# Memory key and value projection woven into the sliding attention's block with its norms, and row norms joined to the projections behind them

## The reference

```python
def memory_kv(mem, lw):
    m = rmsnorm(mem, lw['mem_in_norm_g'])
    k = rmsnorm((m @ lw['w_mk']).reshape(B, M, MEM_HEADS, MEM_HD), lw['mem_k_norm_g'])
    v = (m @ lw['w_mv']).reshape(B, M, MEM_HEADS, MEM_HD)
    return k, v
...
    sq = rmsnorm(sq.reshape(B, T, SWA_HEADS, SWA_HD), lw['swa_q_norm_g'])
    sk = rmsnorm(sk.reshape(B, T, SWA_KV_HEADS, SWA_HD), lw['swa_k_norm_g'])
    h = x + jnp.concatenate([out_a, out_b, out_c], axis=-1) @ lw['w_o']
    h = h + memory_attend(rmsnorm(h, lw['norm_mem_g']), mem_k, mem_v, lw)
    u, ffn_buf_new = causal_dwconv(rmsnorm(h, lw['norm_ffn_g']) @ lw['w_up'], ffn_buf, lw['w_ffn_conv'])
```

## Time and profile before

| | us |
|---|---|
| median of 3 runs | 2190.31 (2185.15 to 2190.46) |
| the profiled execution | 2190.62 |
| its span | 2189.4 |
| TensorE busy | 1968.3 (90%) |
| VectorE busy | 1039.8 (47%) |
| ScalarE busy | 680.0 (31%) |
| GpSimd busy | 530.5 (24%) |

### The profile page before, as it was taken

How to read it: one execution, slowest core, us unless ns; L and a number is a source line. 1 busy time by engine, 2 the same in 40 slices (tenths; PEclk the granted TensorE clock), 3 DMA queues, 4 the chain that set the end, 5 groups by cost and what they waited for, 6 DMA issues and landing times. The chain is left out here.

```text
span 2189.4 us, 28444 instructions
## 1 busy us (share of the span) xinstructions
PE 1968.3 (90%) x10881; PEld 1799.7 (82%) x10881; DVE 1039.8 (47%) x1344; ACT 680.0 (31%) x1216; POOL 530.5 (24%) x453
## 2 busy tenths in 40 slices
PE   3899999889856987699998897999999999999997
PEld 3889889889745776599886687999999999999995
DVE  4224555746542211511341215666666757576665
ACT  4114663226542314311310314322223222222222
POOL 3000221024311606200211502323323223233230
PEclk9999999989976998799999998999999999999998
DMA  3121212141120304210223201212120111112012
GB/s 117 42 61 31 61 30 62 59 137 49 55 74 1 135 10 163 78 39 1 77 97 134 77 1 49 58 29 57 29 57 29 52 34 35 51 29 57 29 39 94
DMA packets 126933, 127.01 MB, mean 58 GB/s; under 512 B 10389, under 2 KB 109310, under 8 KB 126686
## 3 DMA queue, kind: packets, MB, share of 16 engines
q1 hardware_dynamic: 122238, 120.89, 17.8%
q10 hardware_dynamic: 3714, 4.76, 0.7%
q0 software_dynamic: 896, 0.19, 0.0%
HBM read 109.86 MB, written 15.96 MB: 57 GB/s over the span
## 5 line engine op out<-in xcount | busy, mean ns | idle before, releaser
L2732 PE MATMUL ffn_banks<-h_hi,up_hi 128*128 128x384 f32 x1056 | 352.9, 334 | 1.8 <-PEq L116 1.8
L2732 PE MATMUL ffn_banks<-h_hi,up_lo 128*128 128x384 f32 x1056 | 353.0, 334 | 0.0
L2732 PE MATMUL ffn_banks<-h_lo,up_hi 128*128 128x384 f32 x1056 | 352.8, 334 | 0.0
L2907 DVE TENSOR_TENSOR h<-h,ffn_banks 128x512 f32<-128x512 f32 x396 | 272.4, 688 | 146.4 <-PE ffn_banks L2767 142.2
L2877 DVE SCALAR_TENSOR_TENSOR ffn_conv_out<-ffn_conv_in,vec,ffn_conv_out 128x1168 f32<-128x1168 f32 x88 | 206.7, 2349 | 128.3 <-ACT ffn_conv_out L2798 122.5
L706 PE MATMUL proj_banks<-x_hi,in_w_hi 128*128 128x384 f32 (+1 forms) x648 | 222.2, 343 | 4.3 <-DVE room L1071 4.3
L706 PE MATMUL proj_banks<-x_lo,in_w_hi 128*128 128x384 f32 (+1 forms) x648 | 218.1, 337 | 0.0
L706 PE MATMUL proj_banks<-x_hi,in_w_lo 128*128 128x384 f32 (+1 forms) x648 | 217.9, 336 | 0.0
L2732 PEld LDWEIGHTS ffn_banks<-h_hi,up_hi 128*128 128x128 f32 x1056 | 198.2, 188 | 2.9 <-issue 2.0
L2732 PEld LDWEIGHTS ffn_banks<-h_lo,up_hi 128*128 128x128 f32 x1056 | 198.2, 188 | 0.9
L2732 PEld LDWEIGHTS ffn_banks<-h_hi,up_lo 128*128 128x128 f32 x1056 | 198.2, 188 | 0.0
(11 more groups left out here) (395 smaller groups left out, 3501.9 us busy)
## 6 DMA issues: line engine op xcount, KB each, us to landing
up_raw<-in_w_up SPq DMA_DIRECT2D x44, 512.0 KB, 6.2
in_w_raw<-in_w_in SPq DMA_DIRECT2D x22, 512.0 KB, 3.7
down_raw<-in_w_down SPq DMA_DIRECT2D x22, 512.0 KB, 3.7
mem_k_one<-in_cache_mem_k SPq DMA_DIRECT2D x8, 1024.0 KB, 4.9
spill<-mixT SPq DMA_DIRECT2D x10, 576.0 KB, 4.0
wo_w_raw<-in_w_o SPq DMA_DIRECT2D x8, 512.0 KB, 3.8
h<-in_x_prompt SPq DMA_DIRECT2D x8, 512.0 KB, 7.3
mkv_w_raw<-in_w_mk SPq DMA_DIRECT2D x8, 512.0 KB, 4.0
```

Source lines behind the costliest of these rows:

```text
L2732: ins = nc.tensor.matmul(banks[:, NP * s + p, 0:TC], wt[:, s, k, :], x[:, k, TC * p:TC * p + TC], start=(n == 0), stop=(n == 3 * KD - 1))
L2907: nc.vector.tensor_tensor(to, to, banks[:, d_bank[n % 5], :], ALU.add).then_inc(added, 1)
```

## The change

- `late_norms`, `window_attention` and `memory_kv` become one block, `window_and_memory`. In it the memory rows' norm is done beside the key and query norms, and the 192 products of the memory projection are cut into 64 units of three products, which TensorE takes in portions (`UNITS_AT`) between the scores and the outputs of the attention's tiles. One bank takes the groups of eight units one after the other; ScalarE copies each group out (`rows_out`). The weights come in 16 pairs of 128 x 512; ScalarE makes the high parts, GpSimd the low parts of the even pairs, VectorE those of the odd ones.
- The sample tile comes first. Its scores with the old windows are made by 32 products with queries masked for one sequence each, accumulated in the bank.
- Roots in this block are made by log and exp; the key norm gets one refining step on VectorE.
- Turned keys go to memory and are loaded again, with the values, in the block of the query projection.
- `norm_turn` before the query projection and before the FFN goes away; `NormParts` does the same steps inside the product's block. TensorE turns the first eight pieces, and then one piece ahead of each product of the first column; the products of the first column wait for their low part. The first two weight tiles' high parts move from GpSimd to ScalarE, ahead of and in the middle of the norm's high parts. In the query projection the later weights' low parts move from VectorE to GpSimd.
- The FFN's old rows are stored to memory in the input projection and loaded in the FFN's block; masks and buffers share room with others.

The diff, cut. The loops over `NT` at the end of `window_and_memory` are, in this order, those of TensorE, VectorE, ScalarE and GpSimd.

```diff
+class NormParts:
+    GROUP, RING = 3, 4
...
+    def turn(self, pe, i):
+        g, k = divmod(i, KD)
+        pe.wait_ge(self.scaled, self.GROUP * (g + 1))
+        if i >= self.RING:
+            pe.wait_ge(self.low, i - self.RING + 1)
...
+    def on_scalar(self, act, half_way):
+        for i in range(NP * KD):
+            if i == NP * KD // 2:
+                half_way()
+            self.high_part(act, i)
+
+    def on_vector(self, dve):
+        self.inverse(dve)
+        self.scale(dve, 0)
+        for i in range(NP * KD):
+            if i % KD == KD // 2 and i // KD + 1 < NP:
+                self.scale(dve, i // KD + 1)
+            self.low_part(dve, i)
+
+    def first_third(self, pe):
+        for i in range(KD):
+            self.turn(pe, i)
+
+    def before_product(self, pe, p, k):
+        i = KD * p + k + KD // 2
+        if KD <= i < NP * KD:
+            self.turn(pe, i)
+        pe.wait_ge(self.low, KD * p + k + 1)
...
+PAIRS, PAIR_RING, RAW_RING = 2 * KD, 5, 4
+UNITS_FIRST = KD
+UNITS_AT = [(4, 4)] * 5 + [(2, 2)] * 3 + [(4, 0)]
+ROWS_AT = {0: 1, 1: 2, 2: 3, 3: 4, 4: 5, 6: 6, 8: 7}
+PAIRS_FIRST = 4
+PAIRS_AT = {0: (4, 5, 6, 7), 1: (8,), 2: (9, 10, 11, 12), 4: (13, 14, 15)}
+
+def window_and_memory(nc, C, A, O, M, ahead):
+    tile_at = [NT - 1] + list(range(NT - 1))
...
+            def memory_units(n):
+                nonlocal unit
+                for u in range(unit, unit + n):
+                    g, k = divmod(u, KD)
+                    t, j = g % 2, 4 * (g // 2) + k // 2
+                    if k == 0:
+                        if g:
+                            pe.wait_ge(m_copied, g)
+                        else:
+                            pe.wait_ge(m_low, KD)
+                    wait_split(pe, j)
+                    for i, (a, w) in enumerate(((a_hi, w_hi), (a_hi, w_lo), (a_lo, w_hi))):
+                        ins = nc.tensor.matmul(m_flat, a[:, k, P * t:P * t + P], w[:, j % PAIR_RING, k % 2, :],
+                                               start=(k == 0 and i == 0), stop=(k == KD - 1 and i == 2))
+                    ins.then_inc(multiplied, 1)
+                unit += n
...
+            for n in range(4):
+                turn_memory(n)
+            score(0)
+            score(1)
+            memory_units(UNITS_FIRST)
+            for i in range(NT):
+                turn(i)
+                if i + 2 < NT:
+                    score(i + 2)
+                memory_units(UNITS_AT[i][0])
+                output(i)
+                if i == last - 1:
+                    pe.wait_ge(hidden, NT - 1)
+                    turn_keys(0)
+                    turn_keys(1)
+                if i == last:
+                    pe.wait_ge(hidden, NT)
+                    turn_keys(2)
+                    turn_keys(3)
+                memory_units(UNITS_AT[i][1])
...
+            for i in range(NT):
+                if i + 1 < NT:
+                    denominators(i + 1)
+                if i:
+                    output_copy(i - 1)
+                if i + 2 < NT:
+                    maxima(i + 2)
+                for j in PAIRS_AT.get(i, ()):
+                    if j % 2:
+                        weights_low(j)
+                if i == last - 4:
+                    normalize_keys()
...
+            def weights_high(j):
+                act.wait_ge(w_landed[j % RAW_RING], 16 * (j // RAW_RING + 1))
+                if j >= PAIR_RING:
+                    hm, pp = divmod(j - PAIR_RING, 4)
+                    act.wait_ge(multiplied, KD * (2 * hm + 1) + 2 * pp + 2)
...
+            for i in range(NT):
+                if i + 1 < NT:
+                    exponentials(i + 1)
+                copy_turned(i)
+                for j in PAIRS_AT.get(i, ()):
+                    weights_high(j)
+                if i in ROWS_AT:
+                    rows_out(ROWS_AT[i])
+                if i == last - 5:
+                    key_lengths()
...
+            for i in range(NT):
+                b = i % 2
+                pool.wait_ge(inverted, i + 1)
+                nc.gpsimd.tensor_tensor(p[:, b], p[:, b], over(rec[:, b], 256), ALU.mult).then_inc(p_normed, 1)
+                for j in PAIRS_AT.get(i, ()):
+                    if j % 2 == 0:
+                        weights_low(j)
...
@@ query_projection
+            weights.low_parts(nc, pool, n_tiles)
+            norm.first_third(pe)
             for n in range(n_tiles):
...
                     for k in range(KD):
+                        if n == 0:
+                            norm.before_product(pe, p, k)
...
+            norm.factors()
+            weights.high_first(nc, act, 0)
+            norm.on_scalar(act, lambda: weights.high_first(nc, act, 1))
@@ ffn
+                        if s == G and not before:
+                            norm.before_product(pe, p, k)
...
+            sp.dma_start(old[:], C.ffn_old).then_inc(old_landed, 16)
```

More of the change, by code:

```diff
@@ L401, in load_first, with high_first, low_parts @@
             self.load(sp, n)
+    def high_first(self, nc, act, n):
+        self.wait(act, n)
+        nc.scalar.activation(self.hi[:, n], self.raw[:, n], ACT.Copy).then_inc(self.high, 1)
+    def low_parts(self, nc, pool, n_tiles):
+        for n in range(n_tiles):
+            pool.wait_ge(self.high, n + 1)
+            nc.gpsimd.tensor_tensor(self.lo[:, n % 2], self.raw[:, n % self.RING], self.hi[:, n % 2].bitcast(F32), ALU.subtract
+                                    ).then_inc(self.split, 1)
     def split_first(self, nc, pool):
@@ L2209, in row_projection @@
-def row_projection(nc, C, tag, actT, n_tiles, weights, out, sums, residual=None, loaded=False):
+def row_projection(nc, C, tag, actT, n_tiles, weights, out, sums, residual=None, loaded=False, squares=None, stored=None,
+                   stored_too=None):
     A_RING, together = 4, 3
@@ L2280, in sum_of_squares @@
                     act.wait_ge(summed, t)
-                nc.scalar.activation(squares[:], out[:, t, :], ACT.Square, accum_out=sums[:, t:t + 1]).then_inc(summed, 1)
+                elif stored:
+                    act.wait_ge(stored, 16)
+                nc.scalar.activation(squares, out[:, t, :], ACT.Square, accum_out=sums[:, t:t + 1]).then_inc(summed, 1)
             for t in range(together, n_tiles):
@@ L2313, in _, with query_projection @@
                 nc.vector.tensor_tensor(to, to, banks[:, n % 8, :], ALU.add).then_inc(freed, 1)
[L2316 removed]
+def query_projection(nc, C, tag, src, src_sums, gain_col, hi, lo, weights, n_tiles, out, inv_norm, beside):
     RING = weights.RING
@@ L2325, in query_projection @@
         sums = ph.psum(f"{tag}_sums", [P, NT, HEADS])
+        more = ph.psum(f"{tag}_more", [P, 512])
+        norm = NormParts(nc, C, ph, f"{tag}_norm", src, src_sums, gain_col, hi, lo,
+                         out[:].rearrange("p k t -> p (k t)")[:, KD * T - 6 * D:KD * T],
+                         [banks[:, NP + p, :] for p in range(NP)] + [more[:]])
         projected, freed, squared, summed, rooted, inverted = (ph.sem(f"{tag}_{n}") for n in (
@@ L2334, in _ @@
                 weights.load(sp, n)
+            beside(sp)
+        @block.gpsimd
+        def _(pool):
+            weights.low_parts(nc, pool, n_tiles)
         @block.tensor
@@ L2635, in load_first, with ffn @@
         self.load_down(sp, 0)
-def ffn(nc, C, A, O, h, hi, lo, old, weights):
+def ffn(nc, C, A, O, h, hi, lo, weights):
     W = 3
```

744 lines of the change are left out of this document (458 added, 286 removed).

## The result

| | before | after |
|---|---|---|
| median | 2190.39 us | 2127.26 us (2126.19 to 2130.05, 4 runs) |
| the profiled execution | 2190.62 | 2130.05 |
| its span | 2189.4 | 2128.8 |
| TensorE busy | 1968.3 (90%) | 1961.0 (92%) |

The ratio is 0.9719, with a 95% interval of 0.9700 to 0.9738. 2126 was forecast. The total is right; the two terms that it takes off, 58.2 us for the weave and 6.5 us for the joined norms, are not, and their errors cancel.

What follows compares the result with a forecast made beforehand. TensorE was taken to do most work overall, but waits and chains between engines to bind the changed stages. The sum was 2190.6 - 58.2 (weave) - 6.5 (joined norms) = 2125.9, so 2126 us, range 2103 to 2146.

Steps and rivals of the forecast that it cites:

- the weave: Window attention and memory phase: two stages totalling 196.2 us replaced by one woven block of 138 us, giving back 58.2 us.
- the joined norms: Row norms before the query projection and FFN, joined to the products: 1.6 and 4.9 us back, together 6.5 us.
- W: Length of the woven block: 43.5 + 91.5 + 3 for half-clock stretches = 138 us, bounds 122 and 152.
- Start of the block: Woven block up to its first turn: 43.5 us, carried by ScalarE, then the sample tile's scores and softmax.
- the sample's scores: Start of the woven block: 72 records of small TensorE products, taken as 10 us, bounds 7 and 18.
- The slow rival: Woven block: masked scores at half clock throughout (18 us), further 2.5 us stalls in 8-unit tiles; W 158, 2146 us; chance 0.15.
- The nine tiles: Woven block's attention tiles with memory units: 91.5 us, including 5.4 us idle before the fourth turn, 4.0 at the fifth output.
- the eighth needs the fifth low part: FFN join: the eighth transposed piece waits for VectorE's fifth low part, behind a 2.1 us scaling; first product at 1327.6.
- the walk: Step-by-step timing of the joined blocks: first three pieces done after 33 us in the FFN, some 34.5 in the query projection.
- The port contention: Rival: VectorE's low parts and scalings slowed beside GpSimd, on the path, 11 us more or less, 2137 us; chance 0.12.
- The rule of one bank: Memory products share one bank, so groups wait for ScalarE's copy: taken at nothing; seven exposed 0.8 us copies would make 2131.
- The tight weave: Rival: only TensorE binds the woven block, W 122 us, and the norms give 20 us; 2096 us; chance 0.15.

Runs made afterwards that it cites:

- e12: Kernel after with normalisation issued ahead, keys' squares and norms in halves, sample tile third, eight memory units ahead of its scores: 2107.03 us, ratio 0.9621.

## Why the prediction was right, and where it was not

**What is removed and the weave.** Forecast 58.2 us. At the start of the query's block the kernel after is 50.2 us ahead (table load at 850.36, against the root at 900.53 before). Of the missing 8 us, 3.4 lie ahead of the woven block: it began at 600.95, not 597.5, in this slowest of the four runs. In eleven other profiles the same code ended 1.9 to 3.7 us sooner, so this is mostly no effect of the change. W itself was 141.15 instead of 138, the step from the end of the block to the output projection's first product 5.7 instead of 4.9 us, and from there to the query's block 102.6 instead of 102.0.

**Start of the block: 48.65 against 43.5.** The failed term is the sample's scores, 15 us at 0.50 for the 10 that I took between bounds of 7 and 18. With the first prompt tile's scores, 17 us stand for 11 or 12. The slow rival had named the 18, and the sum should have taken one of the two ends: the earlier trace rows showed small products that stayed near half clock for 12 us with no gap. (The 64 small products named for the kernel before are 32, with two records each; the 64 of the earlier trace rows are records.) The first turn came 5.2 us late, which is this term: in the weave it is the step that failed.

**The nine tiles: 92.5 against 91.5 and 3 for the clock.** Right tile by tile, the queues read off the code included: idle 5.73 us ahead of the fourth turn for 5.4, and 2.49 us at the fifth output with ScalarE's copy for 4. The 3 us that were added for the clock weren't needed, and took 2 of the start's 5 us back. The sixth was 2 us longer than forecast, since VectorE's key norms held the copy of an output for 3.15 us, which I had named and not charged.

**The joins: 6.5 forecast, 13.8 measured.** In the FFN the step that failed is "the eighth needs the fifth low part". With four banks the eighth piece takes the bank of the fourth, so it waits for the fourth low part, which VectorE makes ahead of scaling the next group:

```profile
1264.89 4.76 PE L419 MATMUL ffn_banks<-ident,ffn_room 128*128 128x128 f32 x24 [6.40 <-DVE ffn_room L406]
...
1266.66 2.32 DVE L431 SCALAR_TENSOR_TENSOR h_lo<-ffn_banks,vec,h_hi 128x384 fp32r<-128x384 f32 x4 [1.83 <-ACT h_hi L426]
1268.90 2.07 DVE L406 TENSOR_SCALAR ffn_room<-h,nf_inv 128x1024 f32<-128x1024 f32 x3
1269.40 0.42 PE L3036 MATMUL ffn_banks<-h_hi,up_hi 128*128 128x384 f32 x1
...
1275.92 4.23 DVE L406 TENSOR_SCALAR ffn_room<-h,nf_inv 128x1024 f32<-128x1024 f32 x3
...
1280.82 0.52 PE L419 MATMUL ffn_banks<-ident,ffn_room 128*128 128x128 f32 x3 [2.12 <-DVE h_lo L431]
```

The product starts 8.8 us after the block, not 12.4, beside the scaling, and at full clock, as the clock rose during the 24 transposes: 3.6 and 1.9 us gained. Some 3.3 us were lost again further on, part of it at the lower clock (1281.6 to 1285.0). The second scaling took 4.23 us beside GpSimd instead of 2.07, and TensorE stood 2.12 us for the low part behind it. 31.0 us remain for the 33.2 of the walk, 7.1 back instead of 4.9. In the query's block the walk's end was 34.5 us for a measured 31.3, so the join shows as 4.8 us against the kernel before, for the 1.6 forecast. It saves 7.7 us against the 39.0 that the kernel without joins needs there.

**The sum.** 50.2 for the weave, 4.8 and 7.2 for the two joined blocks, less 1.6 in the phases behind them (0.5 up to the FFN's block, 1.1 in its loop), is 60.6 us, the difference of the spans. The forecast was 64.7, and the medians differ by 63.1. The 50.2 us are read at the start of the query's block. The kernel without joins is 52.3 us ahead there and 46.3 at its end: 2.9 go in its query norm, by the table load and the clock, and 3.1 behind it, which I can't place. That two errors of opposite sign, 58.2 for the 48.1 of the weave alone and 6.5 for 13.8, met in a total 1.3 us off is luck.

**The rivals.** Of the slow weave one half came true (scores at half clock throughout), the further stalls didn't. The port contention costs nothing in the weave that the kernel without it shows, and perhaps the 2.1 us of the FFN's join, which no run took out; not 11. It was on the path in the kernel with pair 12 moved, with 1.9 us. The rule of one bank cost nothing: in the tiles 9.0 us apart TensorE doesn't wait for a copy of its group. The tight weave's 122 us for W wasn't reached by the change, but 122 was no lower bound either: with all cures (e12) W is 120.4 us, counted as the 141.15 are, and the weave's length fell from 146.9 to 126.1.

**A faster kernel.** Normalisation ahead, the keys' work in halves, the sample tile third and its scores behind eight memory units: 2107.03 us (2106.12 to 2108.28), 0.9621 of before, 20 us under the kernel after. With the sample fifth it is 2107.52, no different.

## What to carry to other kernels

When work is woven into a chain, write down each engine's queue and look for an item that waits for the woven work and stands ahead of an item that the chain needs. Changing the order of two instructions on GpSimd was worth 9 us, more than the idle time that it removed, since the clock fell in that hole. A hole of 2.3 us brought such a fall in some profiles and none in others, so a difference of 1.5 us between two single profiles may be no more than that.

A norm joined to its product is to be costed against the block as it will stand after the other edits: with what table loaded and at what clock. And a stretch of small products should be priced at each of the two clock levels; here it ran at the level that TensorE had at its start, or fell at once.

## What the runs showed of the hardware

- 72 records of products on 64 rows took 14.5 to 15.1 us at a granted clock of 0.50 and 7.9 us at 1.00. Seven profiles had such a stretch from 0.50 on, without a gap, and none rose in it. Zeros in the stationary tiles made no difference in the one run that tried it. 24 other records on 64 rows saw a rise after 3.5 to 3.8 us in three profiles of four.
- Behind 2.47 us of idle time and a turn at 1.00 the clock fell in the first 0.5 us of these scores; behind 2.38 us, with memory products in their place, it stayed at 1.00. Each is one profile.
- Around an idle time of 2.27 or 2.28 us at the same place of the code the clock fell in three profiles and not in two.
- A two-input VectorE operation on 128 x 4 values took 0.16 us alone and up to 2.28 us beside GpSimd's subtraction. GpSimd's subtraction took 2.4 us alone and 3.36 us beside VectorE's.
